# Other costs in the table that deals a layer's mixing over the expert pairs

## What is computed

```
h  = RMSNorm(x) @ w_in             # u_a, v_a, val_b, gate_b, q_m and three gates
A  = gelu(u_a) * (tril(W_s) @ layernorm(gelu(v_a)) + b)
B  = silu(layernorm(depthwise_conv31(val_b * sigmoid(gate_b))))
M  = attention(q_m, memory keys, memory values)     # samples: cached keys and values
x += (sig(gA)*(A @ W_oA) + sig(gB)*(B @ W_oB) + sig(gM)*(M @ W_oM)) @ w_out
x += PEER(RMSNorm(x))              # 8 heads, 16 of 16384 experts each, by product keys
```

## Time and profile before

| | |
|---|---|
| median of 3 runs | 2243.03 us (2241.05 to 2249.33) |
| profiled execution | 2240.22 us |
| its span, first to last instruction | 2238.2 us |
| TensorE, VectorE, ScalarE, GpSimd busy | 73%, 71%, 29%, 30% |
| bytes moved | 895.54 MB, mean 400 GB/s |
| granted TensorE clock, mean | 0.806 |
| pairs on TensorE: portions 0, 1, 2, 3 begin at | 286, 780, 1351, 1845 us |

### The profile page before, as it was taken

The page is one execution under the profiler, slowest core; times in us unless marked ns, Lnnn a source line. Parts: engine busy times, 40 slices in busy tenths (PEclk is TensorE's granted clock), DMA queues, the critical chain, the costliest instruction groups (busy, mean ns, idle before and its releaser), DMA issues.

```text
span 2238.2 us, 31250 instructions
## 1 busy us (share of the span) xinstructions
PE 1622.8 (73%) x10886; PEld 1056.2 (47%) x10886; DVE 1581.6 (71%) x4231; ACT 659.2 (29%) x1649; POOL 674.7 (30%) x596
## 2 busy tenths in 40 slices
PE   9999987589897367878788647766999854333333
PEld 9965775268675045554444415543888610000001
DVE  3563598778856677877775567977886686776875
ACT  2112234322313242432132323342223333322222
POOL 0000133122232433332223233221323254454443
PEclk9999999689998588999889767886999875555555
DMA  8788999999999999999999999999999999999997
GB/s 310 293 300 292 367 420 421 419 406 420 410 420 418 421 421 421 421 416 422 421 366 421 421 421 413 408 400 402 414 421 421 408 396 421 422 421 422 421 421 326
DMA packets 127771, 895.54 MB, mean 400 GB/s; under 512 B 16096, under 2 KB 16928, under 8 KB 20480
## 3 DMA queue, kind: packets, MB, share of 16 engines
q0 software_dynamic: 83232, 604.02, 65.3%
q1 hardware_dynamic: 44384, 289.54, 32.4%
HBM read 885.39 MB, written 8.11 MB: 399 GB/s over the span
## 4 chain that ended last, share of the span: by engine, by line
PE 35%; DMA 32%; DVE 19%; ACT 5%; issue 4%; DVEq 3%; POOL 1%; SPq 0%; POOLq 0%; ACTq 0%
DMA uv<-uv_in,idx_u 23%; PE bank L1670 16%; DVE uv L1545 9%; DMA ring<-w_in 5%; PE bank L1944 5%; PE bank L2277 5%; PE bank L1676 5%; DMA ring<-cache_in 3%; DVE yB L1038 2%; ACT L611 2%; POOL uv L559 1%; DVE x L1568 1%; ACT diag L942 1%; DVEq L1033 1%; ACT pick L611 1%
## 5 line engine op out<-in xcount | busy, mean ns | idle before, releaser
L559 POOL DMA_INDIRECT uv<-uv_in,idx_u x574 | 658.7, 1147 | 1368.4 <-PE bank L2277 686.8
L1545 DVE CUSTOM_DVE_ANT_0 uv<-uv,xrep 128x1024 f32<-128x1024 f32 x576 | 682.1, 1222 | 205.3 <-DMA uv<-uv_in,idx_u 194.9
L2277 PE MATMUL bank<-uv,diag 128*32 128x512 f32 x2176 | 397.5, 810 | 451.0 <-ACT diag L942 447.5
L1670 PEld LDWEIGHTS bank<-xnT,ring 128*128 128x128 f32 x3168 | 429.3, 200 | 80.8 <-issue 67.4
L1670 PE MATMUL bank<-xnT,ring 128*128 128x160 f32 (+1 forms) x3168 | 450.7, 302 | 4.1 <-DMA ring<-w_in 4.1
L611 ACT ACTIVATE pick<-pick 128x2 f32<-128x2 f32 (+1 forms) x315 | 67.0, 213 | 1064.7 <-DVE pick L1545 1063.0
L2277 PEld LDWEIGHTS bank<-uv,diag 128*32 128x32 f32 x2176 | 50.6, 123 | 637.8 <-ACT diag L942 570.9
L1038 DVE SCALAR_TENSOR_TENSOR yB<-ext_p,small,yB 128x128 f32<-128x128 f32 x960 | 275.1, 348 | 19.9 <-issue 0.4
L611 ACT ACT_TABLE_LOAD x139 | 178.3, 1283 | 2.4
L942 ACT ACTIVATE diag<-gated_fold,pick 128x32 f32<-128x32 f32 x574 | 153.1, 314 | 9.6 <-ACT pick L611 0.3
L1944 PE MATMUL bank<-ring,xnT 128*128 128x512 f32 x192 | 87.4, 610 | 0.0
(11 more groups left out here) (295 smaller groups left out, 1831.5 us busy)
## 6 DMA issues: line engine op xcount, KB each, us to landing
ring<-w_in SPq DMA_DIRECT2D x211, 1024.0 KB
ring<-cache_in SPq DMA_DIRECT2D x32, 1024.0 KB
uv<-uv_in,idx_u POOLq DMA_INDIRECT x578, 13.9
uv<-w_in SPq DMA_DIRECT2D x4, 1024.0 KB, 15.8
ring<-w_in SPq DMA_DIRECT2D x6, 512.0 KB, 6.2
ext_s<-state_in SPq DMA_DIRECT2D x2, 1088.0 KB, 17.0
convs_out<-ext_s SPq DMA_DIRECT2D x2, 1088.0 KB
ext_s<-mem_in SPq DMA_DIRECT2D x2, 1024.0 KB, 14.6
```

Of the source, the lines that this page charges most:

```text
L559: nc.gpsimd.indirect_dma_start(out=uvbuf[2 * b + i], out_offset=None, in_=uv_in, in_offset=bass.IndirectOffsetOnAxis(ap=ids[:, c:c + 1], a ...
L1545: ins = V.tensor_tensor_reduce(out=u, in0=u, in1=xrep[gg % 2][:, :], scale=1.0, scalar=0.0, op0=ALU.mult, op1=ALU.add, accum_out=hid[:, c: ...
L1670: ins = MM(out, w[:, k, P * b:P * (b + 1)], rhs(k), start=k == 0, stop=k == KB - 1)
L2277: ins = MM(vbank[gg % 2][c:c + 32, :], diag[:, t % 4, i], uvbuf[2 * b + i][:, D + 512 * n:D + 512 * (n + 1)], start=first, stop=last)
```

## The change

The costs of the parts are computed by a new function, `share(tensor, pieces)`, from TensorE's time and the number of 1 MB loads of a part: 1.6 times the time less 1.9 per load, and at least 1.2. All the places follow; names and order of the parts stay as they are.

```diff
+def share(tensor, pieces=0):
+
+    return max(1.2, 1.6 * (tensor - 1.9 * pieces))
+
+
 def parts(p):
-    h, across = (3.6, 4.4)[p], (3.5, 4.8)[p]
-    kv = 6.9
+    h, across = share((3.8, 4.6)[p], 1), share((3.8, 5.2)[p], 1)
+    kv, cached, wide = share(6.9, 1), share(1.8, 1), share(7.1, 2)
+    vector, channels = share(1.8), share(2.5)
...
     def S(i):
-        return some("S", 1.2, i)
+        return some("S", share(1.2), i)
 
     def T(i):
-        return some("T", 0.8, i)
+        return some("T", share(0.8), i)
 
     def O(i):
-        return some("O", 1.2, i)
+        return some("O", share(1.2), i)
+
+    def sg(*numbers):
+        return some("sg", share(1.5), *numbers)
...
-        out += some("sk", 2, 0, 1, 2) + O(3) + some("sk", 2, 3, 4, 5, 6, 7) + some("pts", 0.8, 0) + some("va", across, 3)
+        out += some("sk", cached, 0, 1, 2) + O(3) + some("sk", cached, 3, 4, 5, 6, 7) + some("pts", share(0.8), 0) + some("va", across, 3)
...
-        def some_wide(name, *numbers):
-            return some(name, 3.9, *numbers)
-
-        out += some_wide("gt", 0) + some_wide("pr", 0) + [("lng", 1.8)] + some_wide("gt", 1) + [("lnb", 1.8)] + some_wide("pr", 1)
+        out += some("gt", wide, 0) + some("pr", wide, 0) + [("lng", vector)] + some("gt", wide, 1) + [("lnb", vector)] + some("pr", wide, 1)
...
-    out += [("ffn", 1.8), ("tr2", 8)] + some("wq", h, 0, 1) + some("sc", 1, 0) + some("wq", h, 2, 3) + some("sc", 1, *range(1, STEPS[p]))
+    out += [("ffn", vector), ("tr2", 8)] + some("wq", h, 0, 1) + some("sc", 1, 0) + some("wq", h, 2, 3) + some("sc", 1, *range(1, STEPS[p]))
```

More of the change, by code:

```diff
@@ L153, in parts @@
         out += O(0) + T(1) + S(3) + some("va", across, 1) + O(1) + T(2) + some("va", across, 2) + O(2) + T(3)
-        out += some("sk", 2, 0, 1, 2) + O(3) + some("sk", 2, 3, 4, 5, 6, 7) + some("pts", 0.8, 0) + some("va", across, 3)
-        out += some("sv", 2, 0, 1) + some("pts", 0.8, 1) + some("sv", 2, 2, 3, 4, 5, 6, 7)
-        out += some("mg", h / 2, 0) + [("ot", 0.8)] + some("mg", 3 * h / 2, 1)
+        out += some("sk", cached, 0, 1, 2) + O(3) + some("sk", cached, 3, 4, 5, 6, 7) + some("pts", share(0.8), 0) + some("va", across, 3)
@@ L157, in parts @@
+        out += some("sv", cached, 0, 1) + some("pts", share(0.8), 1) + some("sv", cached, 2, 3, 4, 5, 6, 7)
+        out += some("mg", h / 2, 0) + [("ot", share(0.8))] + some("mg", 3 * h / 2, 1)
     if p == 0:
-        def some_wide(name, *numbers):
-            return some(name, 3.9, *numbers)
-        out += some_wide("gt", 0) + some_wide("pr", 0) + [("lng", 1.8)] + some_wide("gt", 1) + [("lnb", 1.8)] + some_wide("pr", 1)
-        out += some("ua", h, 0, 1, 2) + some("sg", 1.5, 0) + some("ua", h, 3) + some("sg", 1.5, 1, 2) + some_wide("gt", 2)
@@ L163, in parts @@
-        out += some("sg", 1.5, 3) + some_wide("gt", 3) + [("csum", 2.5)] + some_wide("pr", 2) + [("csq", 2.5)] + some_wide("pr", 3)
-        out += some_wide("gt", 4, 5) + some_wide("pr", 4, 5) + some("mt", 1.5, 0, 1)
-    else:
-        out += some("mg", h, 2) + [("lng", 1.8)] + some("mg", h, 3, 4) + [("lnb", 1.8)] + some("mg", h, 5, 6, 7) + some("ua", h, 0, 1, 2)
-        out += some("sg", 1.5, 0) + some("ua", h, 3) + some("sg", 1.5, 1, 2) + some("mg", h / 2, 8) + some("sg", 1.5, 3)
-        out += some("mg", 3 * h / 2, 9) + some("mg", h, 10, 11) + [("csum", 2.5)] + some("mg", h, 12, 13) + [("csq", 2.5)] + some("mg", h, *range(14, 24))
+        out += some("gt", wide, 0) + some("pr", wide, 0) + [("lng", vector)] + some("gt", wide, 1) + [("lnb", vector)] + some("pr", wide, 1)
@@ new lines, in parts @@
+        out += some("ua", h, 0, 1, 2) + sg(0) + some("ua", h, 3) + sg(1, 2) + some("gt", wide, 2)
+        out += sg(3) + some("gt", wide, 3) + [("csum", channels)] + some("pr", wide, 2) + [("csq", channels)] + some("pr", wide, 3)
+        out += some("gt", wide, 4, 5) + some("pr", wide, 4, 5) + some("mt", share(1.5), 0, 1)
+    else:
+        out += some("mg", h, 2) + [("lng", vector)] + some("mg", h, 3, 4) + [("lnb", vector)] + some("mg", h, 5, 6, 7) + some("ua", h, 0, 1, 2)
+        out += sg(0) + some("ua", h, 3) + sg(1, 2) + some("mg", h / 2, 8) + sg(3)
+        out += some("mg", 3 * h / 2, 9) + some("mg", h, 10, 11) + [("csum", channels)] + some("mg", h, 12, 13) + [("csq", channels)] + some("mg", h, *range(14, 24))
```

## The result

| | before | after |
|---|---|---|
| median of 22 runs | 2241.58 us (2239.6 to 2249.33) | 2247.16 us (2241.82 to 2252.3) |
| ratio, 95% interval | | 1.0023 (1.0017 to 1.0029) |
| profiled execution | 2240.22 us | 2248.55 us |
| span | 2238.2 us | 2246.5 us |
| share of TensorE, VectorE, ScalarE, GpSimd | 73%, 71%, 29%, 30% | 73%, 70%, 29%, 30% |

The kernel became slower by 5 us where 6.5 us of gain were forecast.

What follows compares the result with a forecast made beforehand. Transfers at about 421 GB/s bound the kernel, with 27 us of lost time within the edit's reach. Terms -6 - 2.5 + 2 = -6.5 us gave 2236.5 us against the median 2243.03; range 2225 to 2248.

Steps and rivals of the forecast that it cites:

- 1120 to 1176, -6: m=2, `gt2` to `pr2`: two more pairs between `gt2` and `pr4` bring back 6 us, bounds 0 and -7.3.
- 2.1 x 4.98 = 10.5 us of transfers there for 2.1 x 1.06 = 2.2 of TensorE: m=2, `gt2` to `pr4`: two more pairs put 10.5 us of transfers there for 2.2 us of TensorE.
- Rival 1: Nothing measurable (-3 to +3): VectorE before `csum` and serial chains set the lost time, not TensorE; 2243 us, chance 0.18.
- 1432 to 1480, -2.5: m=3, queries to `sk0`: one pair more, 5.8 us of transfers, where TensorE waits; 2.5 us gained, bounds 0 and -4.3.
- The first gates, +2: First two gates after cached pieces, 1556 to 1572 and 472 to 496: crowding costs 1 us per layer, bounds -2 and +5.2.
- The tail of m=3, 0: 1776 to 1816, `tr2` to the scores: serial chain, no more loads to cover it; no change, bounds -2 and +2.
- The end of m=2, +0: 1.8 pairs, 9 us of transfers, leave; the queue has enough to spare: no change, bounds 0 and +9.
- its `glu`, 0: `glu` of m=2: at most 42.4 us of TensorE beside 49.3 of transfers, so still covered, no change.
- rival 4: The end of m=2 loses its cover: +9 us on top of the forecast, 2245 us, chance 0.07.
- no effect at all: Whole edit: that it does nothing was excluded, since places change by up to two pairs.
- Rival 2: Balance works everywhere in mixing: dips at 1120, 1432, 584, 1368 and the bursts vanish, 17 us allowed; 2226 us, chance 0.18.
- Rival 3: Crowded cached pieces leave TensorE at half the clock through `mg0` and `mg1`: +13 us over both layers, 2256 us, chance 0.07.

Runs made afterwards that it cites:

- early taps: Kernel before with m=2's new costs, and VectorE doing 15 of the convolution's 62 taps of m=2 earlier, beside `mk0` to `va2`: ratio 0.9998.
- mid group: Kernel before with only m=3's parts `va0` to `sv7` at the pairs the new table gives them: ratio 1.0013.
- the group alone: Kernel before with only m=3's `out0` moved from pair 47 to 46 and `wq0` from pair 51 to 52: ratio 1.0016.

## Why the prediction was wrong

**What held.** That nothing counts but the time in which the transfers run below their rate, and that only 27 us of it are in the table's reach: the stretches of after lie in the three portions, and the head and the last portion are as before (310 and 409 GB/s). That the sum would be small against that. The range held the 2247.16 us, and "within 0.5%" is what came, but by luck: the forecast's sign was wrong, and the loss came from terms that it had small or at nothing.

**Where the sign went.** By portion the forecast had about 6 us of gain for m=2 and 1 for m=3. Alone, m=2's table gave 0.9995, which is 1 us, and m=3's 1.0024, which is 5 us of cost. Two steps failed: what two more pairs give back at 1120, and the price of crowding m=3's cached pieces, its first gates and its tail.

**1120 to 1176, -6: wrong.** The table gave the stretch its two more pairs, and the second portion gained 1.4 to 2.7 us in its lost time, 0.0005 in the ratio, not told from none. The dip itself did not shrink: pairs 49 to 53 lose 5.1 to 6.7 us in the four kernels with m=2's new costs and the old taps, and 2.0 to 6.2 in the thirteen with the old ones. I had noted that VectorE had 55.5 of 65 us ahead of it, and still took 6 of 7.3 for what TensorE's balance would return. The early taps show whose dip it was. What failed is the step "2.1 x 4.98 = 10.5 us of transfers there for 2.1 x 1.06 = 2.2 of TensorE": it priced a pair by TensorE, and VectorE, which each pair also asks for two dots and a share of the picking, was the late engine. Rival 1 had named this, and was right for m=2.

**1432 to 1480, -2.5: right** in kind. TensorE's wait for the piece of `va` fell from 11.4 us to 7.0 in after and 5.7 with m=3 alone. Pairs 12 to 20 lose 0.7 to 3.2 us in the five kernels with m=3's new table (one or two of its places put back in three of them), and 4.4 before: 1.2 to 3.7 us gained.

**The first gates, +2: wrong in place and size.** I priced the burst as one cached piece more. In the whole change the first gates lose 0.1 us (1.4 with m=3 alone), for 3.4 before: the five `sv` pieces and the gates are parted by a pair. The gates alone one pair early cost 8.1 us over pairs 20 to 24, beyond the bound of 5.2 that I had set for two layers. What I did not look at is the step before: between `sk7` and `sv2` stand two serial handovers (scores, VectorE's maximum, ScalarE's exponential, VectorE's norm, transposes), and the pairs between them were their cover. The lists of pairs in the prediction have the cached block at 6.5 to 4.7 pairs, but no term for that: pairs 20 to 24 lost 5.2 us in the profile of after, and the mid group alone cost 1.3 thousandths. Which of its 12 moves does it stays open, since undoing the wait at `pts1` left the ratio at 1.0023.

**The tail of m=3, 0: too small.** The bound was +2. The tail loses 6.2 to 8.3 us in the seven kernels with m=3's new costs (some places or one cost put back in five of them) and 3.9 to 5.7 in those with the old tail, and the group alone is 1.0016 or 3.6 us. I had written down that `wq0` and `wq1` come to stand before one pair, and that nothing covers this chain, and took 0 all the same. But the runs do not put the cost on that pair of parts: `wq0` moved with `pts1` loses 7.1 us at the tail and nothing in the ratio, and `wq0` put back saves nothing. I had no term for `out0`, the group's other move.

**The end of m=2, +0, and its `glu`, 0: right.** Behind 1180 us the second portion loses 0.2 to 0.3 us in the four kernels with m=2's new costs and the old taps. So rival 4 is out.

**Rivals.** What excluded "no effect at all" was understated: three parts of m=2 move by three pairs (`mk1` from 16 to 13), not by up to two. Nothing rests on it. Rival 2 is out: 1120 stayed. Rival 3 had the place nearly right (crowded cached pieces and first gates) and the price wrong in kind. In after the granted clock over the first gates is 0.88, for 0.85 before. That its +13 in the forecast's sum gave 2247.5, next to the 2247.16 measured, is luck. The Trainium skill (TensorE: Matmul & The Clock Gate, section HAM oscillation) speaks of cold starts behind DMA waits. They are there, 4.40 us for 16 matmul records with the gates moved alone against 2.44 in the earlier trace rows, but that is 2 us of a stretch of 30.

## What to carry to other kernels

Where parts are dealt over whole units of other work, a cost table should be compared as the list of parts behind each unit, not as shares: one hair's breadth in a cost moved `pts1` and `wq0` by a pair. Ask of each list how long no unit gets through, and which serial handover has lost its cover; an average of TensorE time per load sees neither. Neither answer is a price yet: a stretch of 22.7 us cost nothing in one kernel, and a wait of 8 us that was taken away gave nothing back in the ratio. And before a dip is given to one engine, take work from the other one there: 15 taps moved closed in one run a dip that two more pairs had left open.

## What the runs showed of the hardware

In slices of 56 us this one core moves at most 420 to 422 GB/s, loads and gathers mixed or gathers alone. The Trainium skill (DMA: Bandwidth & Descriptors, section Where 436 GB/s comes from) gives about 358 GB/s as the limit that binds for reads from HBM, beside a measured 425 for large ones. The runs here agree with the measured one: 421 or 422 in most slices of the page.

A single profiled execution is not enough at this size. The same places lost 0 or 1 to 3 us over the first six pairs from one kernel to the next (422 GB/s from 296 to 320 us with m=1's new table alone, 374 after, with the same parts there), and closing a dip of 6.7 us moved the ratio by nothing that can be told. Why what is saved in the second portion turns up as loss at the start of the third, 4.6 and 5.0 us in the two kernels with m=2's table and early taps, is not settled.
